# Gathered rows of a mixture-of-experts stage turned by VectorE in 32x32 pieces from the eleventh block on

## What is computed

```python
def step(acc, blk):
    e, tok, wt = blk
    xb = h[tok]                                  # gathered rows, 1024 wide
    hb = jax.nn.silu(xb @ we_g[e]) * (xb @ we_u[e])   # 256 wide
    return acc.at[tok].add(wt[:, None] * (hb @ we_d[e]).astype(jnp.float32)), None
```

## Time and profile before

| | us |
|---|---|
| median of 3 runs | 1125.05 (1124.58 to 1125.45) |
| the profiled execution, its own time | 1126.64 |
| span of the profiled execution | 1124.8 |
| PE busy | 1094.1 (97%) |
| DVE busy | 462.7 (41%) |
| ACT busy | 236.4 (21%) |
| POOL busy | 135.3 (12%) |

### The profile page before, as it was taken

The page is one execution under the profiler, slowest core; times in us unless marked ns, Lnnn a source line. Parts: engine busy times, 40 slices in busy tenths (PEclk is TensorE's granted clock), DMA queues, the critical chain, the costliest instruction groups (busy, mean ns, idle before and its releaser), DMA issues.

```text
span 1124.8 us, 16922 instructions
## 1 busy us (share of the span) xinstructions
PE 1094.1 (97%) x6443; PEld 575.1 (51%) x6443; DVE 462.7 (41%) x1286; ACT 236.4 (21%) x516; POOL 135.3 (12%) x163
## 2 busy tenths in 40 slices
PE   6999999999999999999999999999999999999896
PEld 3456677777877545754343443443444444343232
DVE  2218541565456645843274233233232232331157
ACT  4131241222133123211111111111111111111111
POOL 0210000000020010121112112111111121121100
PEclk9999999999999999999999999999999999999999
DMA  9857622021170273899999999999999999999598
GB/s 370 326 207 295 227 79 75 1 85 51 62 266 7 103 255 120 311 365 426 423 425 426 424 417 425 425 416 396 421 409 384 426 399 400 417 391 370 209 412 344
DMA packets 51655, 337.16 MB, mean 300 GB/s; under 512 B 9637, under 2 KB 14089, under 8 KB 30831
## 3 DMA queue, kind: packets, MB, share of 16 engines
q1 hardware_dynamic: 33710, 287.32, 63.0%
q0 software_dynamic: 17856, 48.68, 11.8%
HBM read 311.30 MB, written 37.24 MB: 310 GB/s over the span
## 4 chain that ended last, share of the span: by engine, by line
PE 91%; DMA 4%; DVE 2%; ACT 1%; issue 1%; SPq 0%; DVEq 0%; POOLq 0%; ACTq 0%
PE bank L1561 30%; PE bank L1584 15%; PE bank L1257 10%; PE bank L1276 5%; PE bank L1549 4%; DMA mem<-expert_out_rows 3%; PE bank L1375 3%; PE bank L1376 3%; PE bank L1170 3%; PE bank L1493 3%; PE bank L1254 3%; PE bank L1145 1%; PE bank L1572 1%; PE bank L1340 1%; PE bank L1154 1%; PE bank L1128 1%
## 5 line engine op out<-in xcount | busy, mean ns | idle before, releaser
L1561 PE MATMUL bank<-mem 128*32 128x512 f32 (+2 forms) x1488 | 304.5, 594 | 0.6 <-DVE mem L2247 0.6
L1561 PEld LDWEIGHTS bank<-mem 128*32 128x32 f32 (+2 forms) x1488 | 100.6, 126 | 166.0 <-issue 166.0
L1584 PE MATMUL bank<-mem 128*32 128x512 f32 (+2 forms) x744 | 157.0, 596 | 0.1
L2247 DVE COPY mem<-bank 128x512 f32<-128x512 f32 x48 | 33.2, 691 | 283.3 <-PE bank L1549 283.3
L1257 PE MATMUL bank<-hT,mem 128*128 128x288 f32 x512 | 133.3, 410 | 1.0 <-ACT mem L935 1.0
L1257 PEld LDWEIGHTS bank<-hT,mem 128*128 128x128 f32 x512 | 93.9, 190 | 25.7 <-issue 2.4
L1561 PE MATMUL bank<-x_sb,mem 128*32 128x512 f32 (+2 forms) x416 | 99.3, 594 | 0.0
L1065 ACT ACTIVATE mem<-bank 128x256 f32<-128x256 f32 x48 | 18.4, 384 | 313.0 <-PE bank L1572 312.8
L1584 PEld LDWEIGHTS bank<-mem 128*32 128x32 f32 (+2 forms) x744 | 48.7, 126 | 61.4 <-issue 60.6
L2262 DVE COPY hT<-bank 128x512 f32<-128x512 f32 x48 | 33.2, 691 | 85.7 <-PE bank L1584 85.6
L790 POOL DMA_INDIRECT mem<-ffn_in_rows,idxg x32 | 32.9, 1028 | 264.5 <-DVE idxs L2243 211.0
(11 more groups left out here) (400 smaller groups left out, 1281.2 us busy)
## 6 DMA issues: line engine op xcount, KB each, us to landing
mem<-k_w_exp SPq DMA_DIRECT2D x51, 2048.0 KB, 23.3
mem<-in_w_exp_down SPq DMA_DIRECT2D x51, 1024.0 KB, 22.7
x_sb<-k_w_exp SPq DMA_DIRECT2D x13, 2048.0 KB, 21.4
mem<-k_w_ada SPq DMA_DIRECT2D x8, 2048.0 KB, 9.0
mem<-k_w_in SPq DMA_DIRECT2D x7, 2048.0 KB, 9.7
hT<-in_w_exp_down SPq DMA_DIRECT2D x13, 1024.0 KB, 25.4
mem<-expert_out_rows SPq DMA_DIRECT2D x6, 2048.0 KB, 16.5
mem<-k_w_head SPq DMA_DIRECT2D x4, 2048.0 KB, 18.4
```

The costliest lines, as they stand in the source:

```text
L1561: i = mm(bank[sl, :], xT[:, j % 2, c * BLK + sl.start:c * BLK + sl.stop], wview(r)[0][:, c, :], start=c == 0, stop=c == KC - 1)
L1584: i = mm(ps[4 + hf][sl, :], hhT[:, k * BLK + sl.start:k * BLK + sl.stop], wview(r)[1][:, k, hf * 512:(hf + 1) * 512], start=k == 0, stop=k ...
```

## The change

From block 10 (`TURNED` = 10) on, the gathered rows are no longer turned by TensorE: `x_T(n)` and both `xT_evac(n)` are gone for n of 10 to 47. In their place VectorE runs `turn(n)`: 16 transposing instructions, each of which takes 32 rows x 8 chunks x 32 columns of the gathered rows in SBUF and writes them, turned in 32x32 squares, into `xT`. It stands where VectorE's `xT_evac` stood, between `place` and `gated`. It waits for the gather, and for `up(n - 2)`, which frees its half of `xT`. For those blocks `hh_T(b - 1)` moves between the sixth and the seventh chunk of `up(b)`, from block 9 on. The semaphore `xgT_d` becomes `xT_ready`, and the gathers and `up` wait for that.

```diff
@@ -48,6 +48,7 @@
 XSLOT2 = 4
 OVSLOTS = [0, 1, 3]
 XG = 3
+TURNED = 10
 OVMAX = 4 * U
 DEEP = (T - QS + BLK - 1) // BLK
 RQ = 6
...
@@ -793,9 +792,9 @@
             def ahead(n, q, g):
                 pool.wait_ge(S["idx_ready"], n + 1)
                 if not isinstance(n, int):
-                    pool.wait_ge(S["xgT_t"], n - 1)
+                    pool.wait_ge(S["xT_ready"], n - 1)
                 elif n >= XG:
-                    pool.wait_ge(S["xgT_t"], n - XG + 1)
+                    pool.wait_ge(S["xT_ready"], n - XG + 1)
                 pool.sem_inc(S["pool_step"], 1)
                 gather(q, g)
...
@@ -1083,7 +1081,7 @@
             for b in range(NBK):
                 if b >= 1:
                     hhT_evac(b - 1)
-                if b < NBK - 1:
+                if b + 1 < TURNED:
                     xT_evac(b + 1, b + 1)
                 silu(b, b)
                 if b >= 1:
...
@@ -1536,13 +1534,13 @@
                         i = mm(ps[6][sl, 0:7], Pm[:, j % 2, tt, sl], Re[:, j % 2, tt, si, 0:7], start=tt == 0, stop=tt == NT - 1)
                 i.then_inc(S["idx_mm"], 1)
 
-            def x_T(n, j, s=None):
-
-                g = gbuf(n, j)
-                pe.wait_ge(S[f"gat{g}"], gcount(n, j, s))
-                if not (isinstance(n, int) and n == 0):
+            def x_T(n):
+
+                g = gbuf(n, n)
+                pe.wait_ge(S[f"gat{g}"], gcount(n, n))
+                if n:
                     pe.wait_ge(S["xgT_a"], n)
-                    pe.wait_ge(S["xgT_d"], n)
+                    pe.wait_ge(S["xT_ready"], n)
                 else:
                     pe.wait_ge(S["sh_ready"], NSH - 1)
                 for c in range(KC):
...
@@ -1551,8 +1549,9 @@
 
             def up(n, j, parts, cs=range(KC)):
 
-                pe.wait_ge(S["xgT_a"], n + 1)
-                pe.wait_ge(S["xgT_d"], n + 1)
+                if isinstance(n, int) and n < TURNED:
+                    pe.wait_ge(S["xgT_a"], n + 1)
+                pe.wait_ge(S["xT_ready"], n + 1)
                 if not (isinstance(n, int) and n < 2):
                     pe.wait_ge(S["ehh"], n - 1)
                 bank = ps[7 if j % 2 else 2]
...
@@ -1614,24 +1612,22 @@
             mm(ps[7][:, 0:2 * NE], ones[0:NE, :], sperm[0:NE].rearrange("p a e -> p (a e)"),
                start=True, stop=True).then_inc(S["srt_mm"], 1)
             shared_up(KC // 2)
-            x_T(0, 0)
+            x_T(0)
             shared_up(2)
             find_idx(2, 2, pieces(2))
             assert shared_at == 2 * KC * NSH
             for b in range(NBK):
                 new_gu(b)
-                if b < NBK - 1:
-                    up(b, b, pieces(b))
-                else:
-                    up(b, b, pieces(b), range(KC - 2))
+                split = KC if b + 1 < TURNED else KC - 2
+                up(b, b, pieces(b), range(split))
                 if b == 0:
                     pe.wait_ge(S["tab_ready"], 1)
                 else:
                     hh_T(b - 1)
-                if b == NBK - 1:
-                    up(b, b, pieces(b), range(KC - 2, KC))
-                if b < NBK - 1:
-                    x_T(b + 1, b + 1)
+                if split < KC:
+                    up(b, b, pieces(b), range(split, KC))
+                if b + 1 < TURNED:
+                    x_T(b + 1)
                 if b + XG < NBK:
                     find_idx(b + XG, b + XG, pieces(b + XG))
                 if b >= 1:
...
@@ -2244,7 +2238,20 @@
 
             def xT_evac(n, j):
                 dve.wait_ge(S["xgT_t"], n + 1)
-                cp(xT[:, j % 2, 4 * BLK:8 * BLK], ps[1][:, :]).then_inc(S["xgT_d"], 1)
+                cp(xT[:, j % 2, 4 * BLK:8 * BLK], ps[1][:, :]).then_inc(S["xT_ready"], 1)
+
+            def turn(n, j, s=None):
+
+                g = gbuf(n, j)
+                dve.wait_ge(S[f"gat{g}"], gcount(n, j, s))
+                dve.wait_ge(S["eup"], n - 1)
+                rows = xg[g].rearrange("s (c d) -> s c d", c=KC)
+                cols = xT[:, j % 2, :].rearrange("d (c s) -> d c s", c=KC)
+                for q in range(P // QS):
+                    for a in range(P // QS):
+                        sl, dl = slice(q * QS, (q + 1) * QS), slice(a * QS, (a + 1) * QS)
+                        i = dve.transpose(cols[dl, :, sl], rows[sl, :, dl])
+                i.then_inc(S["xT_ready"], 1)
 
             def gated(n, j):
                 dve.wait_ge(S["egs"], n + 1)
...
@@ -2284,8 +2291,10 @@
             for b in range(NBK):
                 if b + XG < NBK:
                     place(b + XG)
-                if b < NBK - 1:
+                if b + 1 < TURNED:
                     xT_evac(b + 1, b + 1)
+                elif b + 1 < NBK:
+                    turn(b + 1, b + 1)
                 gated(b, b)
                 if b + XG < NBK:
                     idx_out(b + XG, b + XG)
```

More of the change, by code:

```diff
@@ L369, in build @@
             msk_ready pos_mm pos_done tab_ready gu_mm gu_silu sh_ready
-            P_ready idx_mm idx_ready gat0 gat1 gat2 xgT_t xgT_a xgT_d eup egs ehh ehT_t ehT edn eout_a eout_d sct0 sct1
+            P_ready idx_mm idx_ready gat0 gat1 gat2 xgT_t xgT_a xT_ready eup egs ehh ehT_t ehT edn eout_a eout_d sct0 sct1
             ld_gu0 ld_gu1 ld_gu2 ld_gu3 ld_d0 ld_d1 ld_d2 ld_d3 srt_ready srt_mm over yp_mm yh0 yh1 yh2 yh3 yh4 yh5 yh6 yh7 yd_sum yl_sum yf_rt x2_done out_st dch ach pch pool_step""".split()
@@ L645, in _ @@
             sp.wait_ge(S["eup"], max(LASTB[r] for r in range(NE) if slot(r) == XSLOT) + 1)
-            sp.wait_ge(S["xgT_t"], NBK)
+            sp.wait_ge(S["xT_ready"], NBK)
             for t in range(NT):
@@ L659, in last_rows @@
             def last_rows():
-                sp.wait_ge(S["xgT_a"], nov + (NBK + 1))
-                sp.wait_ge(S["xgT_d"], nov + (NBK + 1))
+                sp.wait_ge(S["xT_ready"], nov + (NBK + 1))
                 sp.wait_ge(S["sct0"], 16 * (NBK // 2) + 16 * ((nov + 1) // 2))
@@ L666, in _ @@
             overflow(sp, nov, body, last=last_rows)
-            sp.wait_ge(S["xgT_a"], NBK)
-            sp.wait_ge(S["xgT_d"], NBK)
+            sp.wait_ge(S["xT_ready"], NBK)
             for k in range(2):
@@ L1074, in body @@
                 silu(n, j)
-                xT_evac(n + 1, j + 1)
                 hhT_evac(n)
@@ L1093, in _ @@
             out_rows(NBK - 1, NBK - 1)
-            overflow(act, nov, body, lambda: xT_evac(NBK, NBK))
+            overflow(act, nov, body)
             for i, (t, _) in enumerate(COMBINE):
@@ L1601, in body @@
                 up(n, j, whole)
-                x_T(n + 1, j + 1, s + 1)
                 find_idx(n + 2, j + 2, whole)
@@ L1647, in first_blocks @@
                 find_idx(NBK, NBK, whole)
-                x_T(NBK, 0, 0)
                 find_idx(NBK + 1, NBK + 1, whole)
             def last_done():
-                pe.wait_ge(S["xgT_a"], nov + (NBK + 1))
-                pe.wait_ge(S["xgT_d"], nov + (NBK + 1))
+                pe.wait_ge(S["xT_ready"], nov + (NBK + 1))
                 pe.wait_ge(S["ehh"], nov + NBK)
@@ L1661, in _ @@
             overflow(pe, nov, body, first_blocks, last_done)
-            for name in ("xgT_a", "xgT_d", "ehh", "ehT", "eout_a", "eout_d", "idx_ready"):
+            for name in ("xT_ready", "ehh", "ehT", "eout_a", "eout_d", "idx_ready"):
                 pe.wait_ge(S[name], NBK)
@@ L2266, in body @@
                 gated(n, j)
-                xT_evac(n + 1, j + 1)
+                turn(n + 1, j + 1, s + 1)
                 idx_out(n + 2, j + 2, s + 2)
@@ L2302, in first_blocks @@
                 place_more(NBK + 1, NBK + 1, 1)
-                xT_evac(NBK, NBK)
+                turn(NBK, 0, 0)
                 idx_out(NBK + 1, NBK + 1)
```

## The result

The changed kernel takes 1130.12 us (median of 8 runs, 1127.11 to 1133.51) beside 1125.74 us of the kernel before (8 runs on the same chip, 1124.05 to 1128.0): a ratio of 1.0042 with a 95% interval of 1.0030 to 1.0054. It is 4 to 5 us slower. The prediction was 1124.7 us, no change, with a range of 1109 to 1128. The profiled execution took 1129.81 us, its span is 1128.0.

The account below looks back on a forecast made before the run. TensorE was taken to set the time, with the weight stream barely ahead and its slowest DMA engine full. 1126.64 - 1.3 + 0.9 = 1126.2 us, or 1124.7 against the median 1.59 us lower; range 1109 to 1128.

Parts of the forecast that it names:

- What bounds the kernel: Blocks 10 to 46: TensorE busy 441.95 of 442.00 us, weight loads only 0.7 us (expert 29) and 1.3 us (63) early.
- The slowest DMA engine has no idle time: Weight stream, 590 to 1045 us: slowest engine has 448 to 471 us of work in 455, so landings don't come earlier.
- TensorE's 0.87 us a block: Between `up` and `down`, blocks 10 to 47: each block loses 0.87 us, 33 us of TensorE work in all.
- VectorE's price: `turn` on VectorE: 421 ns per transposing instruction, 6.7 us for 16, with 4.6 to 11.0 us as bounds.
- rival 3: VectorE becomes the bound if `turn` takes over 9.2 us; 1194 us at the upper price; chance 0.10.
- rival 4: Gather late for its earlier use, delaying `gated`, then `up`: 1128 to 1135 us; chance 0.04, shared with more clock falls.
- The clock: Ahead of block 47: a 2 to 4 us wait lowers TensorE's clock; half of 1.7 us counted, 0.9 us.
- Everything else turns into waits ahead of `up`: Blocks 10 to 47: loads cut TensorE's 33 us gain to at most 1.3 us at block 47, the time saved.
- Rival 1: Weight stream not firm: DMA engines even out, winning 9 to 18 us, 1106 to 1115 us; chance 0.14.

Follow-up runs that it names:

- halved stream: Second half of the down weights not loaded for experts 5 to 63: kernel before 1125.59 us, changed kernel 1097.24 us.
- even rows: Rows of each expert's piece filled from the last row down in odd blocks: kernel before 1126.03 us, changed kernel 1113.85 us.
- spare transposes: Kernel before plus 16 VectorE transposes of 32x256 a block in blocks 10 to 47, results unread: 1130.06 us, ratio 1.0042.

## Why the prediction was wrong

**What bounds the kernel**: right. The halved stream left the kernel before where it was and let 28.4 us of the gain through. Waits at blocks 21 and 47 end 0.1 us behind the landings of experts 29 and 63, as said. But these two aren't the only cuts: there are seven waits, the longest, 6.72 us, at block 33, and the first already at 661.67.

**The slowest DMA engine has no idle time**: right, as far as the runs go: with one transpose of 16 the load of expert 63 was issued 6.5 us earlier than before (1022.3) and landed 0.4 us earlier. The reason given for it, more rows on some engines, is borne out by the even rows (landings 4.7 and 5.4 us earlier, and 16 us won by the changed kernel). The prediction used it only to say that landings don't come earlier.

**TensorE's 0.87 us a block**: a little high; 0.79 us a block with the lighter stream, so 30 us and not 33. It changes nothing here, as the stream took it all back (21.5 us of waits and 12.0 of clock).

**VectorE's price**: 421 ns estimated from the rows 7 by size, 436 ns measured, 7.0 us a turn. The range of 0.29 to 0.69 us held it. `turn` is no bound (rival 3): VectorE is busy 358 of 442 us, and with the lighter stream TensorE has no gaps. The gather came in time (rival 4): the group's idle time for its DMA is 0.4 us in all.

**The clock**: 0.9 us were counted for a wait of 2 to 4 us ahead of block 47. The long wait, 3.50 us, came one block sooner, ahead of block 46. The one at block 47 was 1.05 us long, and the windows behind it stay at 1.00, so that it took nothing.

**The step that failed** is "Everything else turns into waits ahead of `up`. ... Saved: 1.3 us", with the landing of expert 63 held at 1043.8 give or take 1.34 us. It landed at 1048.7. The bound on the landing took in one indirect DMA more or less, and had no term for what the change itself does to the stream: VectorE's instructions were costed on VectorE alone. The missing term is 4 to 5 us, measured on its own by the spare transposes (landing 1048.1 instead of 1043.8, 4.4 us of time) and by its removal (landing 1043.4, 1125.16 us against the 1124.7 predicted). Without it the total stands: the changed kernel minus 15 of 16 transposes takes what was forecast. Its parts (1.3 us saved, 0.9 us for the clock) are too small against the noise to be told apart. The same row that showed expert 63 only 1.3 us early should have warned that any delay of the stream beyond 1.3 us is paid one for one: 4.9 us of delay made 3.6. No rival had this mechanism; the one that came nearest in time, the late gather with 1128 to 1135, had another.

**Rival 1**, engines evened out, 1106 to 1115 us, isn't what the change does by itself, but the edit that evens the rows gives 1113.85.

**Open**: what an instruction packet does to its DMA engine. The delay per packet (about 4.4 / 5 = 0.9 us) is more than the packet's own time, 0.31 us in the trace. That the packets are the cause, and not something else that goes with the count of instructions (such as the recording of each instruction for the trace), is argued from the matching counts; no run moved the packets without the instructions. Which engine takes them, and why even rows hide them, isn't shown either.

## What to carry to other kernels

Where a load lands only when all DMA engines have done their part, read its parts and not the mean share: the mean was 0.99 in kernels 16 us apart. Fill the pieces of gathers and scatters so that no engine always gets the full rows; here that alone turned a change that lost 0.4% into one that wins 1.1%. Where weights arrive within a microsecond of their use and one DMA engine is behind the others, count the instructions that a change adds (shown here for VectorE alone), and prefer few long ones: 4 transposes of 1024 a block cost the stream nothing, 16 of 256 cost it 4 us. Here the turn can't be had in longer ones as it is written, since each of its 16 joins another pair of partition quarters.

## What the runs showed of the hardware that was not expected

- VectorE's instruction count reaches the loads: with 608 more instructions and 5 more packets on the instruction queue the last of a load's 16 parts comes 4 to 5 us later; with 1216 more and 9 packets 8.5 us; with 152 long ones it doesn't. With even rows, 608 more instructions made it 0.9 us.
- VectorE's form prices: a transpose of 32x256 in 436 ns, of 32x1024 in 1236 ns, a copy of 32x256 in 284 ns, of 32x8 in 162 ns. So (1236 - 436) / 768 = 1.04 ns per element and some 170 ns on top for a transpose. The estimate by size in the prediction had the same 1.04 ns and 155 ns on top (421 - 266), so it was 15 ns low.
- The 16 transposes of a turn, each starting in another quarter of the partitions than the last, take 7.17 us in a row (VectorE's timeline of after), 16 x 448 ns, 12 ns more than the mean of one: they run one after another, which the prediction's 16 x 421 ns had taken as well.

```profile
807.99 7.17 DVE L2253 STREAM_TRANSPOSE mem<-mem 32x256 f32<-32x256 f32 x16
```

- TensorE's clock answers to short waits: it is at 0.68 and 0.75 in the 6 us behind a wait of 2.99 us, it fell with waits of 2.19, 2.35 and 2.41 us too, and it stayed at 1.00 behind the wait of 1.05 us at block 47.
